# The last residual addition of a two-layer decoder trunk, made by accumulating transfers instead of VectorE

## The reference

```python
for l in range(DEPTH):                                   # DEPTH = 2
    m, c_new, sg_new, sr_new = _mixer(_rmsnorm(h, norm_mix_pre[l]), ...)
    h = h + _rmsnorm(m, norm_mix_post[l])
    f = _swiglu(_rmsnorm(h, norm_ffn_pre[l]), w_gate_up[l], w_down[l])
    h = h + _rmsnorm(f, norm_ffn_post[l])
return h, ...

def _rmsnorm(x, w):
    y = x * lax.rsqrt(jnp.mean(x * x, axis=-1, keepdims=True) + EPS)
    return y * w
```

## Time and profile before

| | us |
|---|---|
| median of three executions | 1368.13 (1368.0 to 1368.16) |
| profiled execution | 1367.97 |
| its span, first to last instruction | 1366.2 |
| PE busy in it | 1351.7 (99%) |
| VectorE | 1016.7 (74%) |
| ScalarE | 674.6 (49%) |
| GpSimd | 116.5 (9%) |
| granted clock of TensorE, mean | 0.996 |
| data moved | 155.91 MB, mean 114 GB/s |

### The profile page before, as it was taken

One profiled execution on the slowest core, in us unless ns is written; L12 is line 12 of the kernel. 1 busy time (PEld: TensorE's weight loads), 2 busy tenths in 40 slices (PEclk: granted clock), 3 DMA queues, 4 the chain that ended last, 5 costly groups with the idle time before them and its releaser, 6 DMA issues.

```text
span 1366.2 us, 29067 instructions
## 1 busy us (share of the span) xinstructions
PE 1351.7 (99%) x12134; PEld 1332.9 (98%) x12134; DVE 1016.7 (74%) x1615; ACT 674.6 (49%) x1360; POOL 116.5 (9%) x175
## 2 busy tenths in 40 slices
PE   9999999999999999999999999999999999999997
PEld 8999999999999999999999999999999999999996
DVE  7746796868999888644586468958689989885545
ACT  5225555547545445544542364635575545455442
POOL 0000212000000000022100012110000000000220
PEclk9999999999999999999999999999999999999999
DMA  5332233121333323477413313321222323324673
GB/s 211 109 109 75 69 112 112 47 86 63 101 116 101 117 93 108 134 221 233 154 62 109 110 62 101 108 95 37 81 94 93 117 100 102 116 97 156 220 231 103
DMA packets 70116, 155.91 MB, mean 114 GB/s; under 512 B 20672, under 2 KB 24128, under 8 KB 69984
## 3 DMA queue, kind: packets, MB, share of 16 engines
q1 hardware_dynamic: 59248, 119.36, 26.5%
q0 software_dynamic: 10448, 34.16, 8.1%
q10 hardware_dynamic: 288, 0.52, 0.1%
HBM read 141.16 MB, written 12.85 MB: 113 GB/s over the span
## 4 chain that ended last, share of the span: by engine, by line
PE 92%; DVE 5%; ACT 1%; issue 1%; DMA 0%; DVEq 0%; ACTq 0%; SPq 0%
PE PS L692 51%; PE PS L1263 8%; PE PS L1262 8%; PE PS L1264 8%; PE PS L699 4%; DVE hT L1958 1%; DVE mT L1957 1%; PE PS L903 1%; DVE Wl L1920 1%; DVE actL L2500 1%; DVE Xl L1937 1%; PE PS L1049 1%; PE PS L1182 1%; PE PS L887 1%; PE PS L875 1%
## 5 line engine op out<-in xcount | busy, mean ns | idle before, releaser
L1334 ACT ACTIVATE Wh<-stage 128x1024 fp32r<-128x1024 f32 x140 | 148.0, 1058 | 290.7 <-PE PS L692 269.3
L692 PE MATMUL PS<-Xh,Wh 128*128 128x260 f32 x1376 | 285.9, 289 | 2.3 <-DVE Wl L1982 1.8
L692 PE MATMUL PS<-Xh,Wl 128*128 128x260 f32 x1376 | 277.5, 283 | 0.0
L692 PE MATMUL PS<-Xl,Wh 128*128 128x260 f32 x1376 | 277.0, 283 | 0.0
L1920 DVE TENSOR_TENSOR Wl<-stage,Wh 128x1024 fp32r<-128x1024 f32 x140 | 171.0, 1222 | 101.8 <-ACT Wh L1334 101.2
L692 PEld LDWEIGHTS PS<-Xh,Wh 128*128 128x128 f32 x1376 | 212.0, 189 | 5.2 <-DVE Wl L1982 2.2
L692 PEld LDWEIGHTS PS<-Xh,Wl 128*128 128x128 f32 x1376 | 212.5, 189 | 0.0
L692 PEld LDWEIGHTS PS<-Xl,Wh 128*128 128x128 f32 x1376 | 212.4, 189 | 0.0
L1262 PE MATMUL PS<-XU,hiA 128*128 128x260 f32 x448 | 126.8, 283 | 0.0
L1262 PE MATMUL PS<-XU,hiB 128*128 128x260 f32 x448 | 126.8, 283 | 0.0
L1263 PE MATMUL PS<-XU,hiA 128*128 128x260 f32 x448 | 126.6, 283 | 0.0
(11 more groups left out here) (391 smaller groups left out, 2871.3 us busy)
## 6 DMA issues: line engine op xcount, KB each, us to landing
stage<-w_slabs SPq DMA_DIRECT2D x143, 512.0 KB, 3.3
raw<-w_slabs SPq DMA_DIRECT2D x136, 256.0 KB, 2.9
dst<-state_ret POOLq DMA_DIRECT2D x32, 256.0 KB, 3.6
dst<-state_gdn POOLq DMA_DIRECT2D x32, 256.0 KB, 4.3
vb<-v_tmp POOLq DMA_DIRECT2D x32, 256.0 KB, 4.7
out_gdn_sample<-dst POOLq DMA_DIRECT2D x16, 256.0 KB, 3.0
out_ret_sample<-dst POOLq DMA_DIRECT2D x16, 256.0 KB, 3.1
hT<-x_t SPq DMA_DIRECT2D x3, 520.0 KB, 6.4
```

What stands on the lines that cost most here:

```text
L692: ins = mm(pj(slot)[:, a], w[:, ws, pos, :], x[:, a, :], start=first and w is Wh and x is xh, stop=last and w is Wl)
L1334: A(weights(G)[0], stage[:, G % NS], ACT.Copy).then_inc(s["hi_split"], 1)
```

## The change

The new semaphore is `h_stored`. When SyncE comes to the ninth slab of layer 1's down projection (n = S_DN + 8), it first waits for the residual of layer 1's mixer and writes all of `hT` to the output in two stores, one for each token half. The last norm of layer 1 multiplies `fT` as before, but no longer adds it to `hT`; the multiplication itself counts up `h_ready`. GpSimd waits after its last state store for the two early stores and then issues the five parts, each when `h_ready` has counted its multiplications: transfers from `fT` to the output with an addition. SyncE's last wait is for all of them. Apart from that two semaphores of the program's first matmuls, `zeros_ready` and `first_rest`, become one, `first_ready`, that counts to two.

```diff
@@ block.sync @@
+                    if l + 1 == DEPTH and n == S_DN + 8:
+                        sp.wait_ge(s["h_ready"], nth_norm(l, 1) + HN)
+                        for a in range(2):
+                            sp.dma_start(yT[:, :, a], hT[:, :, a]).then_inc(s["h_stored"], 16)
                     if l * SLABS + n >= 2:
                         slab(l * SLABS + n)
-            for a, k0, k1 in Y_PARTS:
-                sp.wait_ge(s["h_ready"], nth_norm(DEPTH - 1, 3) + a * KT + k1)
-                sp.dma_start(yT[:, k0:k1, a], hT[:, k0:k1, a]).then_inc(s["y_stored"], 16)
...
+            sp.wait_ge(s["h_stored"], 32)
             sp.wait_ge(s["y_stored"], 16 * len(Y_PARTS))
@@ block.gpsimd, at its end @@
+            pool.wait_ge(s["h_stored"], 32)
+            for a, k0, k1 in Y_PARTS:
+                pool.wait_ge(s["h_ready"], nth_norm(DEPTH - 1, 3) + a * KT + k1)
+                pool.dma_start(yT[:, k0:k1, a], fT[:, k0:k1, a], accum_op=ALU.add).then_inc(s["y_stored"], 16)
@@ block.tensor, first_two @@
-                    pe.wait_ge(s["zeros_ready"], 1)
+                    pe.wait_ge(s["first_ready"], 1)
...
-                    pe.wait_ge(s["first_rest"], 1)
+                    pe.wait_ge(s["first_ready"], 2)
@@ block.vector, new_h @@
-                    step(V.tensor_tensor(src, src, rb[:, a:a + 1].to_broadcast([P, k1 - k0, HC]), ALU.mult))
+                    scaled = V.tensor_tensor(src, src, rb[:, a:a + 1].to_broadcast([P, k1 - k0, HC]), ALU.mult)
+                    if n == 3 and l + 1 == DEPTH:
+                        scaled.then_inc(s["h_ready"], k1 - k0)
+                        return
+                    step(scaled)
                     V.tensor_tensor(hT[:, k0:k1, a], hT[:, k0:k1, a], src, ALU.add).then_inc(s["h_ready"], k1 - k0)
                     dve.wait_ge(s["h_ready"], nth_norm(l, n) + a * KT + k1)
```

More of the change, by code:

```diff
@@ L398, in trunk @@
             "x3_loaded x4_loaded first_loaded slab0_loaded slab1_loaded dst0_loaded dst1_loaded dst0_stored dst1_stored tail_stored "
-            "state_stored y_stored a_stored a_loaded xq_stored x_loaded "
+            "state_stored y_stored h_stored a_stored a_loaded xq_stored x_loaded "
             "tile_done half_done out_sums slab_part x_sums norm_sum ba_done bad_done gst_done rtr_mm rod_mm v_T k_T st_mm sd_mm reads_T "
             "dr_mm dec_mm aT_T kq_mm tO_T y_mm x_mm ks_mm vn_mm qs_mm ds_mm o_mm oT_T dsum_mm row_T kk_mm "
-            "tile_free0 tile_free1 half_free first_added first_rest zeros_ready lo_split h_ready x_ready sq_added wba_ready raw_ready badiag_ready gate_pre "
+            "tile_free0 tile_free1 half_free first_added first_ready lo_split h_ready x_ready sq_added wba_ready raw_ready badiag_ready gate_pre "
             "g_ready g_split conv_done rv_ready rs_ready bv_ready dkin_ready prod_ready mt_ready a_ready xq_ready pt_ready onR_ready "
@@ L1975, in _ @@
                 if l == 0:
-                    V.memset(zeros[:], 0.0).then_inc(s["zeros_ready"], 1)
+                    V.memset(zeros[:], 0.0).then_inc(s["first_ready"], 1)
                     for k in range(KT):
@@ L1981, in _ @@
                             dve.wait_ge(s["hi_split" if k else "first_round"], 1)
-                            V.tensor_tensor(Wl[:, 0, FIRST[k]], stage[:, 0, FIRST[k]], Wh[:, 0, FIRST[k]].bitcast(fp32), ALU.subtract).then_inc(s["lo_split" if k else "first_rest"], 1)
+                            V.tensor_tensor(Wl[:, 0, FIRST[k]], stage[:, 0, FIRST[k]], Wh[:, 0, FIRST[k]].bitcast(fp32), ALU.subtract).then_inc(s["lo_split" if k else "first_ready"], 1)
                     lo(1)
```

## The result

The changed kernel takes 1373.5 us (median of six executions, 1372.8 to 1375.8), the kernel before 1368.1 us: 1.0039 times as long, 95% interval 1.0029 to 1.0049, or 5.4 us more. In a later series it was 1.0043 (1.0029 to 1.0057). The forecast was 1370.2 us in a range of 1366.6 to 1374.0, with a chance of 0.50 for "within 0.2%" and 0.47 for "slower". So the time lies in the range and beyond the border of the case that was called likeliest (1370.9), by 2.6 us; the change costs 5.4 us where 2.1 were forecast.

A forecast was written before the change was run, and what follows sets the result against it. PE held 92% of the waits; the end was VectorE, then transfers. VectorE's 2.85 us won were lost to queued adding transfers, ending 2.05 us later: median 1368.13 becomes 1370.2 us, range 1366.6 to 1374.0.

The forecast's parts named there:

- the case that was called likeliest: Final transfers: each addition costs two copies, giving 1370.2 us; chance 0.42, of which 0.34 below the 1370.9 border.
- Some 0.9 us later the span ends: End of program: the span ends about 0.9 us after the last bytes move, near 1365.3 before the change.
- the four rivals: Second read hides 0.16; GpSimd's descriptor work grows with rows 0.22; adding slower than two copies 0.13; early stores stall PE 0.04.
- the sum of the prediction: End: five parts served in turn, last bytes until 1367.35 instead of 1365.3, so the end is 2.05 us later.
- not near 7.5 us: Failure sign: the span between VectorE's last write and the end, 2.6 us before, should be near 7.5 us.
- VectorE's share: Last norm: without its nine additions VectorE is done at 1360.75 instead of 1363.60, 2.85 us earlier.
- GpSimd's reaction and issue: Final parts: 0.30 us reaction, first bytes about 1.1 us after start, 1.42 in all; each issue 0.55 us.
- rival 2: Final issues: GpSimd's descriptor work grows with rows, up to 2.2 us for 512 rows, giving 1371.8 us; chance 0.22.
- Two copies: Final adding transfers: each costs as much as two copies, 3.2 us for 520 KB, 2.4 for 390, 0.8 for 130.
- Rival 1: Final adding transfers: the second read hides, one copy's time, 1.6 us for 520 KB, giving 1366.7 us; chance 0.16.
- rival 3: Final transfers: adding is slower than two copies; at factor 3 the end is 6.9 us later, 1375.0 us; chance 0.13.
- The middle: Down projection: early stores delay the ninth slab to near 1261, state transfers perhaps 1 us; PE never waits; cost nothing.

## Why the prediction was right or wrong

**The end of the program.** This is the step that failed: "Some 0.9 us later the span ends" was read off SyncE's stores and carried over to GpSimd's. It is 3.5 us in the changed kernel, 2.6 us more, and the runs show such an end four times: 4.4 us with GpSimd's plain stores of the residual, 3.5 with its plain stores of the products, 3.5 in the changed kernel, and 4.5 with 32 KB at the end. The row that would have warned was in the trace of the kernel before: GpSimd's closing instruction lasts until 1346.4, long after its last bytes. None of the four rivals had this cost, and with it the sum of the prediction would have been 1372.8; the last bytes, 0.95 us later than in the sum, make up for the rest to 1373.5, and for 0.2 us more. The last paragraph's "not near 7.5 us" is where it showed: from VectorE's last write to the end it is 11.4 us.

**VectorE's share.** Right in kind, a little more in size: 3.2 us earlier instead of 2.85, since the three multiplications take 2.46 us in all, without the 0.05 us between them and 0.18 us less than their single durations add up to. What this is worth by itself, the run with SyncE's plain stores shows: 1.8 us by its profile.

**GpSimd's reaction and issue.** The reaction of 0.3 us came as read (from 1355.58 + 0.69 = 1356.27 to 1356.57). The 1.42 us from VectorE's write to the first bytes is 0.08 us more than the earlier trace rows give (1340.16 to 1341.5). The first bytes of the first half's second part came 1.83 us after its issue (1356.57 to 1358.4), not 1.1: mis-sized by 0.7 us. The plain stores from GpSimd have their first bytes some 1.3 us after the issue (1361.44 to 1362.7), so part of it is rows and part the adding. This is rival 2 in a small form: not in proportion to the rows (2.2 us for 512), but 0.75 us plain and 1.3 us adding. The 1.3 us pass the 1.2 at which rival 2 put the change over the border, so I was wrong to cost this at nothing; it is 0.65 us of the 3.3 that the sum lacks. At the second half the issues stand behind a busy queue and do not count.

**The rate of the adding transfers.** Right within 0.1 us for 520 KB, as a mean. Two copies were 3.2 us for 520 KB; three blocks (520 KB and 1040 KB) took from 1358.4 to 1368.3, 3.3 us each. The rate is not even within that:

```profile
1358.40:1359.40 1.00, 0.00 (x0) 0.00 (x0) 1.00 (x2) 0.00 (x0) 0.00 (x0) 1.00 1.12 56
1363.60:1367.40 3.80, 0.00 (x0) 0.00 (x0) 0.00 (x0) 0.00 (x0) 0.00 (x0) 0.50 1.24 192
```

The size of the packets is not the reason. The adding transfers go in packets of one row of 1040 bytes (1463 packets for 1.46 MB from 1360.0 to 1368.3), and so do SyncE's plain stores (544 packets for 0.53 MB from 1363.4 on, before the change), which move at 313 GB/s. Rival 1, the hidden second read, is out, and so is rival 3. The changed kernel's last bytes move at 1368.3, against 1367.35 in the sum: 0.65 from the late first bytes, the rest from the rate. The Trainium skill's rule of two reads for one addition ("Collectives: The Full Stack", The bandwidth ceiling) agrees with that time. Whether the transfer really reads twice, no trace here shows. The Trainium skill's rule that many descriptors can be written before the cost of one more shows ("DMA: Bandwidth & Descriptors", Anatomy of one DMA) agrees in part with the plain stores, where 512 rows took 0.2 us more than 128 (0.75 us against 0.55). It says nothing of adding ones, which took 1.3 us.

**The middle.** Right in what it costs, and in all steps but one. The stretches of the changed kernel, against the earlier trace rows:

```profile
1252.00:1254.00 2.00, 2.00 (x19) 2.00 (x18) 1.82 (x4) 1.25 (x5) 0.00 (x0) 1.00 1.07 362
...
1256.00:1258.00 2.00, 2.00 (x19) 2.00 (x18) 0.41 (x1) 1.50 (x3) 0.00 (x0) 1.00 1.08 298
```

The stores fill what was idle. The ninth slab among the transfers issued between 1251 and 1257, with its time to landing:

```profile
stage<-w_slabs SPq DMA_DIRECT2D x1, 512.0 KB, 7.2
```

ScalarE's timeline at that slab's split:

```profile
1262.23 1.06 ACT L1340 ACTIVATE Wh<-stage 128x1024 fp32r<-128x1024 f32 x1 [3.51 <-PE PS L698]
1265.92 1.28 ACT L1862 ACTIVATE vb<-vb,qkvD 128x128 f32<-128x128 f32 x4 [2.63 <-DMA dst<-state_gdn]
```

The slab, issued at 1253.44, lands at 1260.6 (forecast: near 1261), and ScalarE takes it when PE releases the buffer. The step that was off: the state transfers were late by 3.5 us and not by 1. GpSimd's load of the next state is issued at 1261.72 instead of 1258.19, ScalarE waits 2.6 us for it and takes the tenth slab at 1268.26, 6.03 us after the ninth instead of 5.75. The cover of 3.4 us held, by PE's waits and by the run with the early stores alone.

**The chances.** 0.50 for "within 0.2%" hung on a sum that was 0.7 us below the border and had left a term out. The range held since it reached far towards a slower adding, not since it foresaw the cause: that part was luck.

## What to carry to other kernels

Before moving the last transfers of a program, or any last work, to another engine, read how that engine's program ends in the trace: its closing instruction and the wait where all engines meet. A queue is only as cheap as what stands behind it at the end. An adding transfer took twice the time of a plain one here. That cost nothing where other work covered it, and 4 us at the end of the program, where everyone waits for the last bytes. A place where it gains time no run here shows.

## What the runs showed of the hardware that I had not expected

- GpSimd's closing instruction is long whatever came before it. It ends 5.3 to 5.8 us after GpSimd's last instruction where that is a plain transfer (1341.01 to 1346.35 before the change) and also where it is an ordinary addition, some 18 us after the last transfer had landed (1361.39 to 1366.97 with two blocks on GpSimd). So most of its length is no price of a transfer. Where adding transfers were still moving it lasts longer and ends 3.3 us after the last bytes and 8.6 us after the last issue (changed kernel: 1363.0, 1368.3 and 1371.6). What it waits for then, the runs do not settle.
- A plain store of 512 rows costs GpSimd 0.75 us to issue, an adding one 1.3 us, against 0.55 us for 128 plain rows of 2048 bytes and 0.60 us for 128 of 1040 bytes.
- VectorE and GpSimd at work on float32 operations with both inputs in SBUF slow each other down: 0.97 us became 1.99 us on VectorE (780 columns), and with three blocks on GpSimd, 520 columns took VectorE 2.26 us instead of 0.70.
